# Expert hidden values written permuted into one row block, then turned with one transposing instruction per 128 columns

## What is computed

```python
cap = EC_CAPACITY * n_ // N_EXPERTS                      # 2 * 272 // 16 = 34
g, idx = lax.top_k(jnp.swapaxes(aff, 1, 2), cap)
xs = jax.vmap(lambda ub, ib: ub[ib])(u, idx)             # 34 tokens of 1024 per expert
hid = (jax.nn.silu(jnp.einsum('becd,edf->becf', xs, w_gate))
       * jnp.einsum('becd,edf->becf', xs, w_up))         # 34 x 2816
y = jnp.einsum('becf,efd->becd', hid, w_down) * g[..., None].astype(h.dtype)
```

## Time and profile before

| what | us |
|---|---|
| median of 3 runs | 2938.16 (2936.57 to 2940.39) |
| the profiled execution's own time | 2939.95 |
| its span, first to last instruction | 2938.2 |
| PE busy | 2566.5 (87%) |
| VectorE (DVE) busy | 891.5 (30%) |
| ScalarE (ACT) busy | 415.4 (14%) |
| mean DMA rate over the span | 269 GB/s |
| mean granted clock of TensorE | 0.922 of full |

### The profile page before, as it was taken

How to read it: one execution, slowest core, us unless ns; L and a number is a source line. 1 busy time by engine, 2 the same in 40 slices (tenths; PEclk the granted TensorE clock), 3 DMA queues, 4 the chain that set the end, 5 groups by cost and what they waited for, 6 DMA issues and landing times. The chain is left out here.

```text
span 2938.2 us, 45579 instructions
## 1 busy us (share of the span) xinstructions
PE 2566.5 (87%) x20619; PEld 1431.2 (49%) x20619; DVE 891.5 (30%) x1804; ACT 415.4 (14%) x826; POOL 85.3 (3%) x93
## 2 busy tenths in 40 slices
PE   6979579998999998999999999878676889779995
PEld 4524235334444433544444444346665888445553
DVE  1216732301212112131303131027538441242222
ACT  1022100100001000021202121013013221000001
POOL 0001000000000000000000000000000100000000
PEclk9987688999999999999999999989888989889997
DMA  5315335799999998999998999962010005259996
GB/s 178 115 57 192 124 134 216 285 409 386 399 381 375 388 416 350 364 381 403 386 392 360 378 406 394 378 255 93 1 37 1 3 32 190 106 237 423 422 422 277
DMA packets 129434, 789.27 MB, mean 269 GB/s; under 512 B 17473, under 2 KB 19785, under 8 KB 65113
## 3 DMA queue, kind: packets, MB, share of 16 engines
q1 hardware_dynamic: 125785, 773.78, 65.6%
q0 software_dynamic: 3456, 12.58, 1.1%
HBM read 774.79 MB, written 11.53 MB: 268 GB/s over the span
## 5 line engine op out<-in xcount | busy, mean ns | idle before, releaser
L3026 PE MATMUL bank<-ring,arena 128*34 128x512 f32 (+1 forms) x3072 | 692.5, 588 | 71.1 <-DMA ring<-in_w_up 52.7
L3026 PEld LDWEIGHTS bank<-ring,arena 128*34 128x34 f32 x3072 | 185.8, 116 | 477.6 <-issue 456.2
L3052 PE MATMUL bank<-ring,arena 128*34 128x512 f32 (+1 forms) x1536 | 339.4, 559 | 0.7 <-DVE arena L2032 0.7
L3052 PEld LDWEIGHTS bank<-ring,arena 128*34 128x34 f32 x1536 | 106.4, 112 | 184.4 <-issue 146.0
L303 PE MATMUL bank<-arena,ring 128*128 128x256 f32 (+1 forms) x688 | 159.2, 394 | 3.9 <-DVEq L2049 1.8
L303 PEld LDWEIGHTS bank<-arena,ring 128*128 128x128 f32 x688 | 134.1, 195 | 29.5 <-DVEq L2049 2.2
L3509 PE MATMUL bank<-ring,arena 128*64 128x256 f32 x992 | 111.1, 379 | 3.5 <-DMA ring<-in_moe_w_up 2.8
L2023 DVE TENSOR_TENSOR arena<-arena,bank 34x512 f32<-34x512 f32 (+3 forms) x112 | 59.2, 576 | 156.3 <-ACT arena L1095 155.4
L2924 PEld LDWEIGHTS bank<-arena 64*64 64x64 f32 x2304 | 75.7, 139 | 49.5 <-issue 49.5
L313 PE MATMUL bank<-ring,arena 128*128 128x512 f32 (+1 forms) x224 | 98.8, 596 | 0.0
L3038 PEld LDWEIGHTS bank<-consts,arena 34*64 34x64 f32 x1408 | 88.6, 216 | 13.8 <-issue 12.3
(11 more groups left out here) (634 smaller groups left out, 2959.8 us busy)
## 6 DMA issues: line engine op xcount, KB each, us to landing
ring<-in_w_gate SPq DMA_DIRECT2D x128, 1408.0 KB, 13.1
ring<-in_w_up SPq DMA_DIRECT2D x128, 1408.0 KB, 12.9
ring<-in_w_down SPq DMA_DIRECT2D x128, 1408.0 KB, 10.6
ring<-in_w_in SPq DMA_DIRECT2D x46, 1024.0 KB, 7.1
ring<-in_moe_w_down SPq DMA_DIRECT2D x33, 1024.0 KB, 15.4
ring<-in_moe_w_gate SPq DMA_DIRECT2D x31, 1024.0 KB, 13.6
ring<-in_moe_w_up SPq DMA_DIRECT2D x31, 1024.0 KB, 16.0
ring<-in_ada_w SPq DMA_DIRECT2D x24, 1024.0 KB, 7.3
```

The lines of the kernel that those rows point to most:

```text
L3026: last = mm(ps[c][row:row + CAP, 0:n], xsT[:, e, k, :], w[:, at:at + n], start=k == 0, stop=k == KT - 1)
L3052: last = mm(ps[6][row:row + CAP, c:c + n], hidT[:, j, :], w[:, at - m * PIECE:at - m * PIECE + n], start=j == 0, stop=j == FT - 1)
```

## The change

The hidden values of an expert now lie on one row block, partitions 0 to 33, all 2816 of them. Value q * 22 + j is written to column j * 128 + q: within a write, 22 consecutive PSUM elements go to addresses 128 elements (512 bytes) apart, and VectorE reads and writes them so. The banks hold whole groups of 22 (22, 22, 21, 21, 21 and 21 groups: 484, 484 and four times 462 columns), so there are six parts instead of seven. The turn of a block j takes 128 consecutive columns and is one transposing instruction; the two matmuls per block, their step of 22 and their two row blocks are gone.

```diff
         TURNED = FT // 2
-        HID_BANKS = [(c, c * BANK, min(BANK, FF - c * BANK)) for c in range(6)]
+        HID_ROWS = [22, 22, 21, 21, 21, 21]
+        HID_BANKS = [(c, FT * sum(HID_ROWS[:c]), FT * n) for c, n in enumerate(HID_ROWS)]
         DOWN_AT = {2: (0, 1), 3: (1, 2), 4: (2, 4), 5: (4, 5), 6: (5, 7), 7: (7, 8)}
         N_DOWN = FT * D // PIECE
-        HALF_FF = FF // 2
-        HID_PARTS = [(c, max(c * BANK, lo), min((c + 1) * BANK, hi)) for c in range(6) for lo, hi in ((0, HALF_FF), (HALF_FF, FF))
-                     if max(c * BANK, lo) < min((c + 1) * BANK, hi)]
-        hid_by22 = hid[:, 0:HALF_FF].rearrange("p (q j) -> p j q", j=FT)
-
-        def hid_part(at, end):
-
-            row, base = (0, 0) if at < HALF_FF else (SLOT, HALF_FF)
-            return hid[row:row + CAP, at - base:end - base]
+        hid_by_row = hid[0:CAP, :].rearrange("p (j q) -> p q j", j=FT)
+
+        def hid_rows(c):
+
+            q0 = sum(HID_ROWS[:c])
+            return hid_by_row[:, q0:q0 + HID_ROWS[c], :]
+
+        def in_rows(bank):
+
+            return bank.rearrange("p (q j) -> p q j", j=FT)
...
             def silu_act(e):
 
-                for c, at, end in HID_PARTS:
-                    if c == 5:
+                for c, at, n in HID_BANKS:
+                    if c < 5:
+                        act.wait_ge(gate_done, due(act, gate_done))
+                    else:
                         act.wait_ge(piece_used, after(gate_up_pieces[e][KT - 1]))
-                    elif at != HALF_FF:
-                        act.wait_ge(gate_done, due(act, gate_done))
-                    ACTV(hid_part(at, end), ps[c][0:CAP, at - c * BANK:end - c * BANK], ACT.Silu).then_inc(silu_done, up(silu_done))
+                    ACTV(hid_rows(c), in_rows(ps[c][0:CAP, 0:n]), ACT.Silu).then_inc(silu_done, up(silu_done))
...
-                for c, at, end in HID_PARTS:
+                for c, at, n in HID_BANKS:
                     dve.wait_ge(silu_done, due(dve, silu_done))
-                    last = TT(hid_part(at, end), hid_part(at, end), ps[c][SLOT:SLOT + CAP, at - c * BANK:end - c * BANK], ALU.mult)
-                    if end in (FF, (c + 1) * BANK):
-                        last.then_inc(hid_done, up(hid_done))
+                    TT(hid_rows(c), hid_rows(c), in_rows(ps[c][SLOT:SLOT + CAP, 0:n]), ALU.mult).then_inc(hid_done, up(hid_done))
...
                 for f in range(TURNED):
                     g = half * TURNED + f
-                    for row in (0, SLOT):
-                        rows = slice(row, row + CAP)
-                        last = mm(ps[6][row:row + SLOT, f * CAP:(f + 1) * CAP], hid_by22[rows, g, :], ident[rows, rows],
-                                  start=True, stop=True)
+                    last = nc.tensor.transpose(ps[6][:, f * CAP:(f + 1) * CAP], hid[0:CAP, g * P:(g + 1) * P], ident[:CAP, :CAP])
                 last.then_inc(hidT_ready, up(hidT_ready))
```

## The result

The changed kernel takes 2854.32 us (median of 4 runs, 2848.16 to 2856.64) against 2939.27 for the kernel before beside it: a ratio of 0.9709, 95% interval 0.9688 to 0.973. That is 85 us faster. The prediction had 2890 us, 48 us faster, and a range down to 2866; the direction was right, the size was not.

A forecast was written before the change was run, and what follows sets the result against it. PE and DMA were both taken as near their limits, alternating through the ring of six pieces. 46.3 us in the loop + 3.9 at the end - 2 for stepped writes = 48.2 us, giving 2890 us; range 2866 to 2914.

The forecast's parts named there:

- The turn's length: Turn call of an expert: 11 transposing instructions at 72 ns, 0.79 us instead of 2.72, saving 1.93 us a call.
- 3.9 us at the end: Last expert's two turn calls: weights are already there, so both savings are on the path, 3.9 us.
- The factor 0.8: Expert loop: of 58 us PE time saved, 0.8 comes back because the DMA's room is limited and uneven, 46.3 us.
- the low end of the range: All 58 us and the 3.9, no cost, and 10 us for spared half-clock stretches: 2866 us.
- The stepped writes: Silu and multiplication writing with a step: multiplication 5.6 to 7.5 us an expert, 2 us felt in all (0 to 4).
- The clock rival: Behind the 32 turn calls: transposes lower the clock, costing some 44 us, 2934 us, no change to be measured; chance 0.04.
- One by one: Turn call: transposes don't overlap, 272 ns each, 2.99 us a call, 2949 us; chance 0.02.
- Two records a block: Turn call: each transpose runs in two passes, 1.58 us a call, 28 us gained, 2910 us; chance 0.06.
- The DMA did not take it: Rival for the expert loop: the DMA takes all saved time, no return there, 2936 us; chance 0.03.
- The slow multiplication: VectorE's stepped multiplication holds the turn: 2.75 us per 512, 15.1 us for six parts, 2984 us; chance 0.05.

The follow-up runs named there:

- pad_dense: The changed kernel with 8 dense matmuls (128 x 34 stationary, 138 columns moving), output unused, behind the transposes of each turn call; 2912.47 us.
- split_writes: The changed kernel with ScalarE writing silu to consecutive elements on partitions 64 to 97, only VectorE's result stepped; 2854.62 us.
- chain_plus: The changed kernel with a second multiplication of the same form, written to unused partitions, in front of each of the six; 2913.58 us.
- two_pass: The changed kernel with a plain matmul by the identity in place of the transposing instruction; 2926.41 us.
- after: The changed kernel itself, in its first measurement; 2854.32 us.
- pad_transposes: The changed kernel with 24 more transposing instructions, output unused, behind those of each turn call; 2913.73 us.
- before: The kernel before the change, unedited; 2939.27 us.
- plain_writes: The changed kernel with hidden values in natural order, silu and multiplication unstepped, the transposing instruction taking its columns with a step of 22; 2873.68 us.

## Why the prediction was wrong in size

**The turn's length: right, in part by luck.** 0.79 us a call forecast, 0.80 measured; 3.9 us at the end, 4.1 measured; one record per instruction. But the transposes of line 2760 start 62 ns apart at full clock, and their mean of 72 comes from one gap of 255 ns and the last ones at half clock. The changed turn's transposes start 62 ns apart too, and 154 ns pass from the last to the next work. The two errors cancel.

**The failed steps** are three terms of the sum: the clock, which it did not have and which is the largest, the factor of what comes back, and the cost of the stepped writes.

**The factor 0.8: too low.** "From 380 to the best 405 GB/s the DMA has ... 87 us of room", and of the saved 58 us "I take 0.8". The best stretch of a kernel in which the PE holds slots back is no ceiling: 417 GB/s were reached in stretches of the changed kernel, and before the change the DMA already ran at 427 for the 3.4 us around a turn call, shown above. The line above returns 0.92 of what the PE is spared. The plainest single case is pad_dense, with 7 us more of half clock than the changed kernel: 32 x 2.0 = 64 us of PE time more and 58 us slower (64 by the ratios). Worth 7 to 9 us of 58.

**The clock: the term that was missing, and the main failed step.** The sum had nothing for it; the low end of the range took "10 us in case the shorter turn also spares some of the half-clock stretches". It spares 68 us of them in the profiled executions, 34 us of PE time (20 to 34 by the clocks of all runs). I had the 0.96 in front of me and the fall behind line 2760's transposes, and used them only for a rival in which the changed turn would lower the clock. The question that was not asked is which work lowers it now. One cut of the kernel before around a turn call, shown above, would have answered it. With 34 us in the sum and 0.92 to 0.95 for the factor, (58 + 34) x 0.92 + 3.9 = 89 us to 91 us, less the next term.

**The stepped writes: length right, cost low.** 5.6 to 7.5 us forecast for the multiplication, 5.87 measured. The parts of that sum were not right: the same parts without a step take 3.46 us, the stepped write adds 0.57 ns an element and the stepped read 0.28, where 0.69 had been taken for each. "I take 2 us in all" for what is felt: the PE's waits for it rose from 6 to 16 and 20 us, and taking the step off silu and off the read (split_writes) gave some 6 us back. I had looked only at the distance to the turn call (the tightest, 547.9 - 545.86, is 2.0 us and not 2.1); the waits are in front of it, bank by bank at the first row tile. What these 10 to 14 us of wait cost lies between 4 us, at chain_plus's rate, and their full length. That makes 75 to 87 us of gain, and 77 to 85 were measured. The terms were read from the same runs, so this only shows that they are enough and is no test of them.

**The rivals.** The clock rival went the other way round. One by one: the starts are 62 ns apart with a duration of 224, so it is out. Two records a block did not happen, and its price was wrong by 16 us: such a kernel takes 2926, not 2910. The DMA did not take it: its rate rose by 6%. The slow multiplication did not come: a part takes 1.0 us where 2.1 would have decided. chain_plus came near that (12.4 us an expert, 12.8 would have decided) and is 53 us slower than the changed kernel, yet still 26 faster than the kernel before.

## What to carry to other kernels

When a stretch is full of matmuls with few columns, price it twice: by its own length, and by the granted clock of the microseconds behind it. Cut the trace there before the change is costed; here the second price was a third to more than half of the first. The best transfer rate of a stretch in which another engine holds the buffers back is no ceiling for the transfers. And to turn fp32 data on the PE, a transposing instruction is worth far more than the halved count of records: with everything else equal it took 0.80 us where plain matmuls by the identity took 2.57.

## What the runs showed of the hardware

- Half-clock stretches came behind turn calls of 2.3 to 2.8 us made of small matmuls or transposes (10 to 19 of them in 32 calls), and hardly behind calls of 0.8 us (1 or 2), nor behind 0.8 us of transposes followed by 2.0 us of dense matmuls (0). Dense matmuls added behind the full former turn, or mixed into it, did not prevent them. What exactly the chip looks at is not shown.
- Plain fp32 records with 34 x 128 stationary and 34 columns moving start 112 ns apart (two_pass), transposing ones of the same shape 62 ns (after, pad_transposes). Plain ones with 34 x 64 stationary, taken in turns from partitions 0 to 33 and 64 to 97, start in pairs about 123 ns apart (before).
- Small matmuls (34 x 64 stationary) and dense ones (128 x 34) in turns pay at every change: with four dense matmuls between the small ones a call took 0.8 us more than with the same four behind them (4.71 against 3.87 us).
- Writes with a step of 512 bytes on 34 partitions cost ScalarE 1.04 us instead of some 0.55 for a part of 462 to 484 elements, and VectorE 5.07 us for an expert instead of 3.46 (plain_writes), 5.87 if it reads with the step too. A stepped read costs VectorE half as much as a stepped write.
